# Two hybrid layers, a mixture of experts and a Mamba layer on one core: tiles on 64-byte lines, input first, modulation rows moved, wider compression products, keys of two branches projected once

## The reference

```python
for l in range(2):                                   # first block
    h = rmsnorm(x, norm1_g[l])
    x = x + hybrid_mixer(h, ...)                     # HGRN and GLA linear attention, NSA sparse attention, gated mix
    h = rmsnorm(x, norm2_g[l])
    x = x + swiglu(h, ...)
x = rmsnorm(x, final_norm_g)
for layer in range(2):                               # second block
    mod = silu(c) @ ada_w[layer] + ada_b[layer]      # 6 x 1024: shifts, scales, gates
    h = modulate(rmsnorm(x, norm1_w[layer]), shift1, scale1)
    x = x + gate1 * (pool and chunk attention if layer == 0 else mamba2)(h)
    h2 = modulate(rmsnorm(x, norm2_w[layer]), shift2, scale2)
    x = x + gate2 * hier_moe(h2, ...)                # 32 experts of width 128
return rmsnorm(x, final_norm_w)
```

## Time and profile before

| | |
|---|---|
| median of 3 runs | 2392.18 us (2391.69 to 2393.94) |
| the profiled execution | 2398.61 us, of which the span of instructions is 2396.8 us |
| granted TensorE clock, mean | 0.919 |
| busy: PE, DVE, ACT | 2130.4 us (89%), 1472.9 us (61%), 1045.1 us (44%) |
| matmuls | 16,970 |
| L293, L290 (594 units) | 1,223 ns and 1,046 ns each |
| HBM read | 368.07 MB, 154 GB/s over the span |

### The profile page before, as it was taken

The page is one execution under the profiler, slowest core; times in us unless marked ns, Lnnn a source line. Parts: engine busy times, 40 slices in busy tenths (PEclk is TensorE's granted clock), DMA queues, the critical chain, the costliest instruction groups (busy, mean ns, idle before and its releaser), DMA issues. The chain is left out here.

```text
span 2396.8 us, 40348 instructions
## 1 busy us (share of the span) xinstructions
PE 2130.4 (89%) x16970; PEld 2022.8 (84%) x16970; DVE 1472.9 (61%) x2373; ACT 1045.1 (44%) x1465; POOL 0.2 (0%) x4
## 2 busy tenths in 40 slices
PE   6879888999979787989996687999979898899997
PEld 5878867999978777889995677999979877799997
DVE  3757555687868564657876555555548654465554
ACT  3643434454355433435442334444446553344443
POOL 0000000000000000000000000000000000000000
PEclk9889888999989887989998888999989998899999
DMA  4333322588944233235887313555525321355552
GB/s 152 124 114 106 115 75 94 170 304 301 321 143 133 89 106 106 89 128 199 323 307 261 132 61 106 174 180 177 176 88 169 131 79 54 123 167 176 179 176 95
DMA packets 101269, 371.73 MB, mean 155 GB/s; under 512 B 11489, under 2 KB 11745, under 8 KB 100705
## 3 DMA queue, kind: packets, MB, share of 16 engines
q1 hardware_dynamic: 99936, 364.78, 45.1%
q10 hardware_dynamic: 1152, 4.38, 0.5%
HBM read 368.07 MB, written 1.05 MB: 154 GB/s over the span
## 5 line engine op out<-in xcount | busy, mean ns | idle before, releaser
L293 DVE TENSOR_TENSOR low<-raw,high 128x1024 fp32r<-128x1024 f32 x594 | 725.3, 1223 | 492.6 <-ACT high L290 489.5
L290 ACT CAST high<-raw 128x1024 fp32r<-128x1024 f32 x594 | 618.4, 1046 | 577.0 <-PE ps L358 554.5
L356 PE MATMUL ps<-hh,high 128*128 128x256 f32 x2864 | 838.2, 293 | 26.3 <-PEq L589 11.2
L357 PE MATMUL ps<-hh,low 128*128 128x256 f32 x2864 | 823.3, 287 | 0.0
L358 PE MATMUL ps<-hl,high 128*128 128x256 f32 x2864 | 822.1, 287 | 0.0
L356 PEld LDWEIGHTS ps<-hh,high 128*128 128x128 f32 x2864 | 560.6, 196 | 45.4 <-issue 38.4
L357 PEld LDWEIGHTS ps<-hh,low 128*128 128x128 f32 x2864 | 561.0, 196 | 0.5 <-issue 0.5
L358 PEld LDWEIGHTS ps<-hl,high 128*128 128x128 f32 x2864 | 559.4, 195 | 0.0
L356 PE MATMUL ps<-ffn_high,high 128*128 128x256 f32 x672 | 190.0, 283 | 3.8 <-DVE ffn_low L1864 2.4
L357 PE MATMUL ps<-ffn_high,low 128*128 128x256 f32 x672 | 187.5, 279 | 0.0
L358 PE MATMUL ps<-ffn_low,high 128*128 128x256 f32 x672 | 187.4, 279 | 0.0
(11 more groups left out here) (427 smaller groups left out, 2898.0 us busy)
## 6 DMA issues: line engine op xcount, KB each, us to landing
raw<-in_stream SPq DMA_DIRECT2D x594, 512.0 KB, 3.4
ada_rows<-in_ada SPq DMA_DIRECT2D x96, 512.0 KB, 5.3
bias<-in_bias ACTq DMA_DIRECT2D x1, 1536.0 KB, 6.0
xT<-in_xT ACTq DMA_DIRECT2D x1, 1024.0 KB, 6.5
c_act<-in_c SPq DMA_DIRECT2D x2, 512.0 KB, 5.1
out<-xT SPq DMA_DIRECT2D x1, 1024.0 KB, 3.9
par<-in_par SPq DMA_DIRECT2D x1, 858.0 KB, 4.7
hybrid_const<-in_const ACTq DMA_DIRECT2D x1, 800.0 KB, 5.6
```

The source lines that it names most:

```text
L290: return act.copy(self.high[:, slot, :], self.raw[:, slot, :])
L293: return dve.tensor_tensor(self.low[:, slot, :], self.raw[:, slot, :], self.high[:, slot, :].bitcast(F32), ALU.subtract)
L356: pe.matmul(out, sh, mh, start=start, stop=False, **more)
L357: pe.matmul(out, sl, mh, start=False, stop=False, **more)
```

## The change

1. **Tiles.** `sb` puts a filler tile behind every tile whose size is not a multiple of 64 bytes. `xT`, `hh`, `hl` and `sq` now start at multiples of 128 bytes, `ffn_high`, `hidden_high_half` and `z_high` still 64 past one, the ring's tiles where they were.
2. **Start.** x comes in four chunks at the head of SP's queue, raw unit 0 behind the second. ACT's queue brings only the first norm's gains, then the constants; the other parameters come later. The `ACTIVATE` of L818 is gone. The first block has its own order on DVE, ACT and PE.
3. **Keys.** `nks` and `nkw` become one product `nkk` of two units, undoubled; two units fewer in a layer (590 in all), which leaves two places of the second linear attention's table empty. The query's heads are laid out by group, so heads 0 to 3 lie on partitions 0 to 63 and heads 4 to 7 on 64 to 127; `rope` has four turns. The compressed scores go to a bank for each group.
4. **Compression.** All 64 matmuls of the first compression matrix are 256 columns wide, over windows that overlap; ACT copies 192 columns more for each of the two.
5. **Modulation.** Layer 1's 48 rows and their `finish` move into the first mixture of experts; the 48 rows of layer 0 are dealt out over the gate and up products of the two SwiGLUs, 24 in each. The down products have none. `modulated_gains` of layer 0 goes into the block of the sum of squares, that of layer 1 to the end of the mixture.
6. **Entries.** In an entry behind a residual, the split of x stands ahead of the last unit's low part and no longer behind it.

The core of the diff:

```diff
         def sb(name, shape, scope=everywhere, dt=F32):
-            return scope.enter_context(nc.sbuf_tensor(name, shape, dt))
+
+            tile = scope.enter_context(nc.sbuf_tensor(name, shape, dt))
+            short = -((4 * math.prod(shape[1:]) + 31) // 32 * 32) % LINE
+            if short:
+                scope.enter_context(nc.sbuf_tensor("after_" + name, [P, short // 4], F32))
...
         def first_loads(sp):
-            for i in range(RING):
+            for c in range(KD // 2):
+                sp.dma_start(xT[:, 2 * c:2 * c + 2, :], x_in[:, 2 * c:2 * c + 2, :]).then_inc(x_loaded[c], 16)
+                if c == 1:
+                    ring.load(sp, 0, 0)
+            for i in range(1, RING):
                 ring.load(sp, i, i)
             for i in range(RING):
                 sp.wait_ge(ring.split.sem, i + 1)
                 ring.load(sp, RING + i, i)
 
         def first_parameters(act):
-            act.dma_start(xT[:, :, :], x_in).then_inc(x_loaded, 16)
-            for l in range(DEPTH):
-                act.dma_start(par1[:, l, :], par1_in[l, :, :]).then_inc(x_loaded, 16)
+            act.dma_start(par1[:, 0, 0:KD], par1_in[0, :, 0:KD]).then_inc(gains_loaded, 16)
             act.dma_start(const[:, :], const_in[:, 0:N_KEPT]).then_inc(loaded, 16)
             act.dma_start(lb[:, :], lb_in).then_inc(loaded, 16)
 
```

The entry, on PE and on DVE:

```diff
+                    product(pe, 0, u, 1, None)
                     pe.wait_ge(loaded, 16 * 2)
-                    for c in range(KD // 2 - 1):
+                    for c in range(KD // 2):
                         self.add_sums(pe, c)
-                self.add_sums(pe, KD // 2 - 1)
-                product(pe, 0, u, 1, None)
-                self.spread(pe)
-                for j in range(1, EARLY):
+                    product(pe, 1, u, 0, None)
+                    self.spread(pe)
+                    product(pe, 1, u, 1, None)
+                else:
+                    self.add_sums(pe, KD // 2 - 1)
+                    product(pe, 0, u, 1, None)
+                    self.spread(pe)
+                    product(pe, 1, u, None, None)
...
-                        res.add(dve, j)
-                        res.prod.after_read(dve, j)
-                    else:
+                if res is None:
+                    dve.wait_ge(gains_loaded, 16)
+                    dve.wait_ge(x_loaded[0], 16)
+                    self.weigh(dve, 0)
+                    dve.wait_ge(x_loaded[1], 16)
+                    self.weigh(dve, 1)
+                    self.split(dve, 0)
+                    first_split(dve, 0)
+                    for j in range(2, KD // 2):
+                        dve.wait_ge(x_loaded[j], 16)
+                        self.weigh(dve, j)
+                        self.split(dve, j - 1)
+                    self.split(dve, KD // 2 - 1)
+                    for j in range(1, RING):
                         first_split(dve, j)
-                        if j == 0:
-                            dve.wait_ge(x_loaded, 16 * (1 + DEPTH))
+                    bounds_differences(dve)
+                for j in range(KD // 2 if res is not None else 0):
+                    units = list(res.prod.units_of(j))
+                    for i in units[:-1]:
+                        res.unit(dve, i)
+                    res.add(dve, j)
+                    res.prod.after_read(dve, j)
                     self.weigh(dve, j)
-                    if res is not None:
-                        res.unit(dve, units[-1])
                     self.split(dve, j)
-                if res is None:
-                    bounds_differences(dve)
-                if res is not None and res.mods is not None:
-                    res.mods.finish(dve)
+                    res.unit(dve, units[-1])
                 self.column(dve)
```

Compression, scores, and the windows:

```diff
+        def wide(i, j):
+
+            at = j * 2 * (2 * NCMP + 2)
+            return flat((fh, fl)[i][:, 12:22, :])[:, at:at + T]
...
-                            pe.matmul(ps[:, 4 + i, 0:2 * cols], wh, both[i][:, j, :], start=(j == 0), stop=False,
-                                      skip_group_check=True)
-                            ins = pe.matmul(ps[:, 4 + i, 0:cols], wl, both[i][:, j, 0:cols], start=False,
-                                            stop=(j == 2 * BLOCKS - 1), skip_group_check=True)
+                            pe.matmul(ps[:, 4 + i, 0:T], wh, wide(i, j), start=(j == 0), stop=False)
+                            ins = pe.matmul(ps[:, 4 + i, 0:T], wl, wide(i, j), start=False, stop=(j == 2 * BLOCKS - 1))
...
+                        n = 15 * 2 * cols + T - 16 * 2 * cols
+                        act.copy(flat((fh, fl)[i][:, 12:22, :])[:, 16 * 2 * cols:16 * 2 * cols + n], W[:, i, 0:n])
                         tell(act.copy(both[i][:, :, 0:cols], win[i]), to_dve)
...
 
+        def group_query(h, t):
+
+            lo = h // 4 * NSA_DH
+            return qk[lo:lo + NSA_DH, h % 4, t * P:(t + 1) * P]
...
                         for h in range(NSA_H):
-                            lo, g = h % 2 * NSA_DH, h // 4
-                            at = t * P + h // 2 * 32
-                            ins = pe.matmul(ps[:, 4 + h % 2, at:at + NCMP], query_half(h, qk, t),
+                            g, lo = h // 4, h // 4 * NSA_DH
+                            at = t * P + h % 4 * 32
+                            ins = pe.matmul(ps[:, 4 + g, at:at + NCMP], group_query(h, t),
```

Modulation:

```diff
             def vector(self, dve, upto):
 
-                for i in range(self.dealt, min(upto, ADA)):
...
                         dve.wait_ge(c_ready.sem, c_ready.base + 1)
-                    dve.wait_ge(ada_full[i % 2], self.full0 + 16 * (i // 2 + 1))
+                    row = self.lo + i
+                    dve.wait_ge(ada_full[i % 2], 16 * (row // 2 + 1))
                     r = self.rows[:, i % 2, :]
                     dve.scalar_tensor_tensor(r, r, 1.0, self.c[:, :], ALU.mult, ALU.mult,
-                                             accum_out=self.now[:, i:i + 1]).then_inc(ada_used.sem, ada_used.one())
+                                             accum_out=mod[:, row // ADA, row % ADA:row % ADA + 1]) \
+                        .then_inc(ada_used.sem, ada_used.one())
...
+            def rows(i):
+                return min(max((i - 11) * ADA // 80, 0), ADA)
+
             with new_block() as block:
                 @block.sync
                 def _(sp):
-                    w.sync(sp)
+                    for i in range(w.n):
+                        w.sync(sp, [i])
+                        if mods is not None:
+                            mods.sync(sp, rows(i))
...
                         if s > LAG and s % 2 == 0 and s <= E_N:
                             rest_of_hidden(s // 2 - 1)
+                        if s >= LAG and mods is not None:
+                            mods.vector(dve, rows(down_at(s - LAG)))
+                    if mods is not None:
+                        mods.finish(dve, 1)
+                        modulated_gains(dve, 1)
```

More of the change, by code:

```diff
@@ L571, in add_squares @@
                 pe.matmul(ps[:, 4, 0:T], ones, sq[:, k, :], start=(k == 0), stop=(k == KD - 1))
-        def sum_of_squares():
-            with new_block() as block:
-                @block.scalar
-                def _(act):
-                    for c in range(KD // 2):
-                        square_tiles(act, c)
-                @block.tensor
-                def _(pe):
-                    for c in range(KD // 2):
-                        add_squares(pe, c)
         def rms_norm(gain, shift=None, out=None, width=D, load=None):
@@ L1577, in _ @@
                     cos, sin = (C(n).unsqueeze(1).broadcast_to([P, 2, T]) for n in ("cos", "sin"))
-                    for j in range(5):
+                    for j in range(4):
                         x = qk[:, 2 * j:2 * j + 2, :]
@@ L1827, in sync @@
                     sp.dma_start(self.c[:, :], c_in).then_inc(c_loaded, 16)
-                for i in range(self.loads, min(upto + 2, ADA)):
+                for i in range(self.loads, min(upto + 2, self.n)):
                     self.loads = i + 1
                     if i >= 2:
-                        sp.wait_ge(ada_used.sem, self.used0 + i - 1)
-                    sp.dma_start(self.rows[:, i % 2, :], ada_in[self.layer * ADA + i, :, :]).then_inc(ada_full[i % 2], 16)
+                        sp.wait_ge(ada_used.sem, self.lo + i - 1)
+                    sp.dma_start(self.rows[:, i % 2, :], ada_in[self.lo + i, :, :]).then_inc(ada_full[i % 2], 16)
@@ L1834, in scalar @@
             def scalar(self, act):
-                act.wait_ge(c_loaded, 16 * (self.layer + 1))
+                act.wait_ge(c_loaded, 16 * (self.turn + 1))
                 tell(act.activation(self.c[:, :], self.c[:, :], ACT.Silu), c_ready)
             def vector(self, dve, upto):
-                for i in range(self.dealt, min(upto, ADA)):
+                for i in range(self.dealt, min(upto, self.n)):
                     if i == 0:
```

(31 more changed lines are left out.)

107 lines of the change are left out of this document (50 added, 57 removed).

## The result

The changed kernel takes 2359.05 us, median of 4 (2357.92 to 2361.51), against 2393.06 us before (2391.69 to 2397.58): a ratio of 0.9856, 95% interval 0.9839 to 0.9873, that is 30 to 39 us less, 34 by the medians. The forecast was 2351, in a range of 2306 to 2366.

The account below looks back on a forecast made before the run. PE, never idle in the SwiGLU's gate and up products and the mixture, was taken as the bound there, with waits for DVE at the start and down products' ends. Terms summed to -41 from 2392.2, giving 2351 us, range 2306 to 2366.

Parts of the forecast that it names:

- the likeliest case: Whole kernel: the summed terms give 2351 us, own range 2342 to 2361, chance 0.48.
- Rows of layer 0's down product: Layer 0's down product and next entry: without modulation rows, PE's wait for the split goes; -15 us, bounds 12 to 17.
- Rows at layer 1's end: End of layer 1's down product: without rows the adds follow PE's last product closely; -12 us, bounds 9 to 15.
- Start: Kernel start: first matmul at 8.5 to 10.5 us, row copy near 32; -11 us, bounds 7 to 17.
- Rows in the mixture: First mixture of experts: 48 added modulation rows stay hidden beside its units; 0 us, bounds 0 to +20.
- rival (c): First mixture: becomes bound by transfers, slower than before, at a rate under 251 GB/s; chance 0.02.
- Keys: Second linear attention and rope: 96 fewer matmuls priced at zero, one rope turn fewer 0.9 a layer; -2 us.
- rival (d): Second linear attention: the keys' saving is real, 11 us in all, 2340; inside the likeliest range, which has chance 0.48.
- Compression: Compression: 256-column products may keep the granted clock at 1.00; -1 us a layer, bounds -2.5 and +1.
- Scores: Compressed scores: four heads in turn in one half of the partitions; 0 us, upper bound +3.2 a layer.
- Entries: Entries with a last low part: the split of x ahead of it; -1 us over all, bounds -2 and +1.
- Tiles: `hh` matmuls: at a multiple of 128 bytes they get 0.3 to 0.6 ns slower; +2.5 us, bounds -43 and +4.

Follow-up runs that it names:

- e6: The changed kernel with the 48 modulation rows in the mixture left out, layer 0's columns taking their place; 2357.3 us, ratio 0.9849.
- e5: The changed kernel with the compressed scores' heads alternating between the halves of the partitions, layout unchanged; 2366.2 us, ratio 0.9879.
- e8: The changed kernel with the compression products narrow again, at 64 and 32 columns; 2370.0 us, ratio 0.9891.
- e7: The changed kernel with the last unit's low part ahead of the split of x again in the entries; 2362.6 us, ratio 0.9865.
- e1: The changed kernel without the filler tiles, so hh stands at 96 modulo 256 bytes again; 2352.8 us, ratio 0.9826.
- e2: The kernel before with the filler tiles alone added; 2407.0 us, ratio 1.0051.
- e3: The changed kernel with fillers ahead of the moving tiles, so that all start at 64 modulo 256 bytes; 2321.4 us, ratio 0.9695.
- e4: The changed kernel with the ring's tiles 64 bytes further, every other tile where it was modulo 256; 2339.9 us, ratio 0.9772.

## Why the prediction was right

The number lies in the range, 8 us above the forecast, and the likeliest case came: none of the rivals did. The forecast of -41 against the 40.7 of the traces is closer than its terms are, and that part is luck: the start, the keys and the end of layer 1 gave some 8 us more than forecast, the tiles, the mixture and the scores took at least as much back. Step by step:

- *Rows of layer 0's down product*, -15: 15.4. The entry behaved as the first layer's own.
- *Rows at layer 1's end*, -12, and the block fewer, -0.5: 15.4. The mechanism was right and each part a little larger: short waits of PE inside the product 1.9 us (1.4 forecast), the lateness of the adds 8.0 (7.2), what followed them in the block 4.1 (3.5), the blocks behind 1.5 (0.5).
- *Start*, -11: 15.0, within 7 to 17. The first matmul came when forecast (10.44; 8.5 to 10.5). What I undersized is the pace: I gave 1.4 us to a PE that reaches it earlier, and it reached it before the sums, which alone saved 3.0.
- *Rows in the mixture*, 0: it cost 3.3 us (e6), within 0 to 20. 276 GB/s were moved with PE at 50.00 of 50; rival (c) needed a rate under 251 where 296 were wanted.
- *Keys*, -2: 3.2 by the two ropes alone; the 96 matmuls beside the linear attention gave nothing (the split in front of it and that behind it moved alike, by 16.0 us), as forecast against rival (d).
- *Compression*, -2: 8.3 to 7.4 us a layer, 1.8 in sum, as forecast. But one reading under it was wrong: the passes of the earlier trace rows that I took for ones at 1.00 ran at 0.50 (e5). And the fall seen before was of 15 matmuls, and I priced only those; e8 shows that without wide products the changed kernel falls in them for 37.
- *Scores*, 0, bound +3.2 a layer: +0.9 a layer. Here the rule of the Trainium skill (TensorE: Matmul & The Clock Gate, Part 3) was right in its direction where I took zero.
- *Entries*, -1: 0.9 by the trace of e7, in the whole time not seen.
- **Tiles, +2.5, bounds -43 and +4: this is the term that failed.** The step was "that is the nearest row", 118.8 ns of `early_high_start`. `hh` came to 119.8, outside what I thought possible on that side, and the tiles cost 6 (e1) to 13 us (e2). The place on a line was the wrong variable. With the places modulo 256, all seven paces of the trace of before would have been in one table, and `early_high_start` is at -128 from the ring, not at 0 as `hh` was to be. Such a table would have shown that no pair of that trace stands at 0: the nearest rows were not near, and the 119.8 could not have been read from them.
- *Taking the difference over to the median.* The profiled execution of before stood 6.4 us above the median, and the 40.7 of the traces are 34 of the medians. That is most of the 8 us by which the number is off.

## What to carry to other kernels

Where PE is never idle, measure the distance between its matmuls' starts for each pair of tiles, and write beside it where the stationary and the moving tile stand modulo 256 bytes: here a few hundred bytes of filler were worth 38 us, and "aligned", distance 0, was among the slowest places. Transfers dealt out beside a full PE must fit the rate of their own stage, not the kernel's mean; 24 rows stood beside each down product, and some 15 us went where they went; the 48 that now stand in the mixture cost 3.3 us. Where the granted clock falls some 40 times in a kernel, a microsecond is read in its own stage and not in the total.

## What was not expected of the hardware

- The pace of three-fold fp32 products at 2.4 GHz depends on the distance between the stationary and the moving tile modulo 256 bytes: 113.3 ns for most of the time at -64, 119.8 at 0, the others between; shown by moving either (e3, e4). Whether 256 bytes is the whole period was not tested, and two steady paces at one distance stay unexplained.
- After a wait PE often goes on at 213 ns a matmul, at a granted clock of 0.50, mostly for 12 to 27 matmuls; before layer 0's compression alone, in the same program, these came to 123 to 145 matmuls, and over a whole run the changed kernel and e5 differ by 87 of them, some 8 us.
- Products of 64 and 32 columns let the granted clock fall to 0.50 within a compression of 64 of them (six of six stages), products of 256 columns in their place did not (none of 22).
